# A decoder kernel on one core: the preparation of sparse attention in another order

## What is computed

```python
q, rows, win, gates, qm = nsa_split(hp @ nsa_w_in[j], nsa_gate_b[j])     # 12 query heads, 2 kv heads, head size 128
q = rms_norm(q, nsa_g_q[j])                                              # q / rms(q) * g_q
kc = rms_norm(nsa_compress(rows[:, :, 0], ...), g_k[0])                  # 3 kinds of keys, each normed
ks, kw = rms_norm(rows[:, :, 2], g_k[1]), rms_norm(win_k, g_k[2])
s = einsum(q, k) * HEAD_DIM ** -0.5 + table[t5_bucket(dist)]             # in each of three branches
o = gate_0 * o_cmp + gate_1 * o_sel + gate_2 * o_win                     # gates are sigmoids
```

## Time and profile before

| | us |
|---|---|
| median of three runs | 3449.14 (3446.73 to 3450.45) |
| the profiled execution | 3445.69, of which the span on the core is 3443.8 |
| `prepare_sparse` | from 674.4 to 728.9 |
| `attend_sparse_prompt` | from 728.9 to 815.8 |
| `attend_sampled` | from 815.8 on |
| busy over the span: TensorE, VectorE, ScalarE, GpSimd | 92%, 47%, 37%, 6% |

### The profile page before, as it was taken

How to read it: one execution, slowest core, us unless ns; L and a number is a source line. 1 busy time by engine, 2 the same in 40 slices (tenths; PEclk the granted TensorE clock), 3 DMA queues, 4 the chain that set the end, 5 groups by cost and what they waited for, 6 DMA issues and landing times. The chain is left out here.

```text
span 3443.8 us, 56594 instructions
## 1 busy us (share of the span) xinstructions
PE 3169.4 (92%) x23855; PEld 2974.5 (86%) x23855; DVE 1612.0 (47%) x1681; ACT 1275.7 (37%) x1312; POOL 204.1 (6%) x137
## 2 busy tenths in 40 slices
PE   7899999875679999999999999967699999999999
PEld 6798999844349999999999999944299999999999
DVE  5543444346764544334444444365745443344433
ACT  5432345324763433333332432245034332334332
POOL 0000000003430000000000000025100000000000
PEclk9999999978989999999999999978799999999999
DMA  6556454324754455455555445304644555555553
GB/s 219 156 160 206 139 157 136 122 98 141 234 193 159 146 160 171 160 171 160 170 160 171 149 161 169 106 25 142 214 146 141 166 164 166 165 165 164 165 166 132
DMA packets 317556, 541.82 MB, mean 157 GB/s; under 512 B 18277, under 2 KB 115551, under 8 KB 316136
## 3 DMA queue, kind: packets, MB, share of 16 engines
q1 hardware_dynamic: 316728, 534.45, 48.1%
q10 hardware_dynamic: 624, 4.46, 0.3%
HBM read 519.59 MB, written 27.55 MB: 159 GB/s over the span
## 5 line engine op out<-in xcount | busy, mean ns | idle before, releaser
L516 DVE TENSOR_TENSOR project_weights_low<-ring_x,project_weights_high 128x2048 fp32r<-128x2048 f32 x344 | 788.6, 2292 | 1207.0 <-ACT project_weights_high L444 1206.9
L444 ACT ACTIVATE project_weights_high<-ring_x 128x2048 fp32r<-128x2048 f32 x344 | 658.7, 1915 | 1256.8 <-PE project_banks L372 1256.8
L370 PE MATMUL project_banks<-high,project_weights_high 128*128 128x288 f32 x2560 | 761.6, 297 | 27.6 <-DVE project_weights_low L506 23.8
L371 PE MATMUL project_banks<-low,project_weights_high 128*128 128x288 f32 x2560 | 760.2, 297 | 0.0
L372 PE MATMUL project_banks<-high,project_weights_low 128*128 128x288 f32 x2560 | 759.9, 297 | 0.0
L370 PE MATMUL project_banks<-up_high,project_weights_high 128*128 128x288 f32 x2048 | 605.4, 296 | 0.0
L371 PE MATMUL project_banks<-up_low,project_weights_high 128*128 128x288 f32 x2048 | 605.2, 296 | 0.0
L372 PE MATMUL project_banks<-up_high,project_weights_low 128*128 128x288 f32 x2048 | 605.1, 295 | 0.0
L370 PEld LDWEIGHTS project_banks<-high,project_weights_high 128*128 128x128 f32 x2560 | 486.8, 190 | 29.3 <-DVE project_weights_low L506 24.5
L371 PEld LDWEIGHTS project_banks<-low,project_weights_high 128*128 128x128 f32 x2560 | 486.3, 190 | 0.0
L372 PEld LDWEIGHTS project_banks<-high,project_weights_low 128*128 128x128 f32 x2560 | 485.3, 190 | 0.0
(11 more groups left out here) (516 smaller groups left out, 3021.2 us busy)
## 6 DMA issues: line engine op xcount, KB each, us to landing
ring_x<-in_w_up_dram SPq DMA_DIRECT2D x128, 1024.0 KB, 5.2
ring_x<-in_w_down_dram SPq DMA_DIRECT2D x128, 1024.0 KB, 5.1
ring_x<-in_gla_w_in_dram SPq DMA_DIRECT2D x40, 1024.0 KB, 5.0
h<-in_cache_nsa_kv_dram SPq DMA_DIRECT2D x256, 128.0 KB, 2.3
ring_x<-in_w_out_dram SPq DMA_DIRECT2D x32, 1024.0 KB, 5.1
ring_x<-in_nsa_w_in_dram SPq DMA_DIRECT2D x28, 1024.0 KB, 5.0
ring_x<-in_w_mem_kv_dram SPq DMA_DIRECT2D x16, 1024.0 KB, 5.2
sp_keys_values<-in_cache_nsa_kv_dram SPq DMA_DIRECT2D x64, 256.0 KB, 3.8
```

Of the source, the lines that this page charges most:

```text
L370: nc.tensor.matmul(bank, w_high, moving_high[:, kt], start=(kt == 0), stop=False)
L371: nc.tensor.matmul(bank, w_high, moving_low[:, kt], start=False, stop=False)
L444: nc.scalar.activation(weights_high[:, c % 2], g.ring[:, c % RING], ACT.Copy).then_inc(rounded, 1)
L516: nc.vector.tensor_tensor(weights_low[:, c % 2], g.ring[:, c % RING], weights_high[:, c % 2].bitcast(F32), ALU.subtract).then_inc(split, 1)
```

## The change

In `prepare_sparse` the order of SP's loads is turned round (`near` last). The 24 prompt query tiles are turned by TensorE, in six sets of four placed between the sets of rows, and ScalarE squares each set out of PSUM; VectorE sums them along the free axis, where 24 matmuls did so before. The key squares and their sums come first. The sampled queries are copied to `q_sampled` early and raw; ScalarE squares and multiplies them by the gain. Their inverse norm is applied in `attend_sampled`, where VectorE's additions of a bias become scalar_tensor_tensor with the scale `q_scale_sampled`. The flips come last.

```diff
+        TURNS = [("rows", n) for n in range(4)] + [("queries", n) for n in range(3)] + [
+            ("rows", 4), ("queries", 3), ("rows", 5), ("queries", 4), ("rows", 6), ("queries", 5), ("rows", 7), ("rows", 8)]
 # sync
-            sp.dma_start(g.near[:], ...).then_inc(loaded, 16)
+            sp.dma_start(gate_rows[:], a.gate_rows).then_inc(loaded, 16)
+            sp.dma_start(g.sparse_masks[:], a.sparse_masks).then_inc(loaded, 16)
             sp.dma_start(bias[:], g.bias_dram).then_inc(loaded, 16)
-            sp.dma_start(g.sparse_masks[:], a.sparse_masks).then_inc(loaded, 16)
-            sp.dma_start(gate_rows[:], a.gate_rows).then_inc(loaded, 16)
+            sp.dma_start(g.near[:], ...).then_inc(near_loaded, 16)
...
 # tensor
+            for at, (what, n) in enumerate(TURNS):
+                if at == 3:
+                    pe.wait_ge(k_squared, 1)
+                    for o in range(KEYS):
+                        mm = nc.tensor.matmul(sums_ps[32 * o:32 * o + 32, 3, 0:TOKENS], g.ones[:, 0:32], squares[:, o], ...)
+                    mm.then_inc(k_summed, 1)
+                rows(n) if what == "rows" else queries(n)   # rows waits rows_copied n-3, queries q_squared n-2
+            pe.wait_ge(own_squared, 1)
+            for t in range(PAIRS):
+                mm = nc.tensor.matmul(sums_ps[:, 3, OWN_AT + t:OWN_AT + t + 1], own_squares[:, t], g.ones[:, 0:1], ...)
...
+            pe.wait_ge(k_inverse, 1)
+            pe.wait_ge(q_squared, Q_SETS)
+            pe.wait_ge(q_mean, 1)
+            pe.wait_ge(blank, 1)
+            for o in range(KEYS):
+                mm = nc.tensor.matmul(sums_ps[:, o, 0:TOKENS], spread[:, o], inverse_rms[:], start=True, stop=True)
+            mm.then_inc(spread_done, 1)
+            pe.wait_ge(near_loaded, 16)
             for n in range(FLIPS):   # waits gates_read, scaled, flip_copied 1; banks of rows_ps and sums_ps in turn
...
-            for k in range(HEADS):
-                for i in range(QT):
-                    nc.tensor.matmul(rows_ps[:, 2, k * QT + i:k * QT + i + 1], q_squares[:, k, i * P:(i + 1) * P], ...)
 # scalar
-            nc.scalar.activation(q_squares, g.p[:, 0:HEADS], ACT.Square).then_inc(q_squared, 1)
+            for at, (what, n) in enumerate(TURNS):
+                rows(n) if what == "rows" else queries(n)   # Copy to g.rows, or Square of sums_ps to q_squares
+                if at == 4:
+                    act.wait_ge(own_copied, 1)
+                    nc.scalar.activation(own_squares[:], g.q_sampled[:], ACT.Square).then_inc(own_squared, 1)
+                    act.wait_ge(own_squared, 1)
+                    nc.scalar.activation(g.q_sampled[:], g.q_sampled[:], ACT.Copy, scale=g.vec[:, gq:gq + 1])
+                if at == 6:
+                    act.wait_ge(k_mean, 1)
+                    nc.scalar.activation(inverse_rms[:], inverse_rms[:], ACT.Sqrt).then_inc(k_root, 1)
+            act.wait_ge(q_mean, 1)
+            nc.scalar.activation(q_rms[:], q_rms[:], ACT.Sqrt).then_inc(q_root, 1)
             for n in range(FLIPS):   # copies, now from flip_ps[n]
...
 # vector: neg_bias; key squares; the 16 copies; k_mean; gates; key gains; k_inverse; then
+            for n in range(Q_SETS // 2):
+                dve.wait_ge(q_squared, 2 * n + 2)
+                linked(nc.vector.tensor_reduce(q_rms[:, 8 * n:8 * n + 8], ..., AX_X, ALU.add))
 # then q_mean; gates read; q_scale, q_scale_sampled; the keys scaled (scaled); the bias read; new_k
-            linked(nc.vector.scalar_tensor_tensor(own, own, scaled_gain[:, 0:1], q_rms[:, HEADS * QT:]..., ALU.mult,
-                ALU.mult))
 # attend_sampled, vector (L2146; L2154, L2226, L2232 and L2235 in the same way)
-                linked(nc.vector.tensor_tensor(s_cmp[:], s_ps[:, 0]..., cmp_bias[:]..., ALU.add))
+                for t in range(PAIRS):
+                    last = nc.vector.scalar_tensor_tensor(s_cmp[:, t], s_ps[:, 0, t * P:(t + 1) * P], q_scale(t),
+                                                          cmp_bias[:], ALU.mult, ALU.add)
+                linked(last)
```

More of the change, by code:

```diff
@@ L1398, in _, with rows @@
         def _(pe):
-            for n, (s, tok) in enumerate(sets):
-                if n >= 4:
-                    pe.wait_ge(rows_copied, n - 3)
+            def rows(n):
+                s, tok = sets[n]
+                wait(pe, rows_copied, n - 3)
                 for o in range(4):
@@ L1442, in sum_squares @@
[L1442 to L1461, removed]
@@ L1476, in _ @@
                     g.near[:].rearrange("p h c -> p (h c)").rearrange("p (n b c) -> p n b c", b=FLIP_BANKS, c=512)[:, n],
[L1477 to L1482, removed]
+                    flip_ps[n], ACT.Copy).then_inc(flip_copied, 1)
+            act.wait_ge(own_gained, 1)
         @block.vector
@@ L1504, in _ @@
             nc.vector.tensor_reduce(g.gates_sampled[:], own_gates[:].rearrange(
-                "p (r t c) -> p t r c", t=PAIRS, c=2 * STEP), AX_X, ALU.add)
-            dve.wait_ge(turned, len(sets) + 2)
+                "p (r t c) -> p t r c", t=PAIRS, c=2 * STEP), AX_X, ALU.add).then_inc(gates_read, 1)
+            dve.wait_ge(q_root, 1)
+            linked(nc.vector.reciprocal(q_rms[:], q_rms[:]))
+            nc.vector.tensor_scalar(g.q_scale[:].rearrange("p k i -> p (k i)"), q_rms[:, 0:UNITS], SCALE, None, ALU.mult)
+            nc.vector.tensor_scalar(g.q_scale_sampled[:], q_rms[:, UNITS:], SCALE, None, ALU.mult)
+            dve.wait_ge(spread_done, 1)
+            dve.wait_ge(rows_turned, len(sets))
+            for o, (tile, gain) in enumerate(normed):
+                parts = [(slice(0, SEQ), key_gain[:, gain - gk:gain - gk + 1]),
+                         (slice(SEQ, TOKENS), g.vec[:, gain:gain + 1])]
+                for cols, col in parts:
+                    last = nc.vector.scalar_tensor_tensor(g.p[:, tile, cols], g.p[:, tile, cols], col,
+                                                          sums_ps[:, o, cols], ALU.mult, ALU.mult)
+            last.then_inc(scaled, 1)
+            dve.wait_ge(biased, 1)
             nc.vector.tensor_copy(g.bias_far[:], rows_ps[:, 3, 0:1])
@@ L1516, in _ @@
                     linked(nc.vector.scalar_tensor_tensor(g.bias_near[:], near, at, g.bias_near[:], ALU.mult, ALU.add))
[L1517 to L1536, removed]
@@ L1545, in _ @@
-            for r in range(rounds):
-                dve.wait_ge(root, r + 1)
-                nc.vector.reciprocal(inverse_rms[:, r % 2], inverse_rms[:, r % 2]).then_inc(inverse, 1)
-                dve.wait_ge(spread_done, r + 1)
[L1549 to L1553, removed]
-                    parts = [(slice(0, SEQ), key_gain[:, gain - gk:gain - gk + 1]),
-                             (slice(SEQ, TOKENS), g.vec[:, gain:gain + 1])]
-                    for cols, col in parts:
-                        last = nc.vector.scalar_tensor_tensor(g.p[:, tile, cols], g.p[:, tile, cols], col,
-                                                              sums_ps[:, o, cols], ALU.mult, ALU.mult)
-                last.then_inc(scaled, 1)
@@ L1560, in _ @@
[L1560 to L1568 removed]
+            nc.vector.tensor_scalar(g.bias_far[:], g.bias_far[:], 1.0, None, ALU.mult).then_inc(bias_read, 1)
@@ L2152, in front @@
                 yield -1.5
-                for w in range(2):
-                    last = nc.vector.tensor_tensor(
-                        s_new[:, :, w], s_ps[:, 1, 0:2 * PAIRS * NEW].rearrange("p (t w n) -> p t w n", w=2, n=NEW)[:, :, w],
-                        mask[:, SP_OTHER:SP_OTHER + PAIRS * NEW].rearrange("p (t n) -> p t n", n=NEW), ALU.add)
+                for t in range(PAIRS):
+                    other = mask[:, SP_OTHER + t * NEW:SP_OTHER + (t + 1) * NEW]
+                    last = nc.vector.scalar_tensor_tensor(
+                        s_new[:, t], s_ps[:, 1, 2 * t * NEW:2 * (t + 1) * NEW].rearrange("p (w n) -> p w n", n=NEW),
+                        q_scale(t), other.unsqueeze(1).to_broadcast([P, 2, NEW]), ALU.mult, ALU.add)
                 last.then_inc(small_taken, 1)
```

156 lines of the change are left out of this document (92 added, 64 removed).

## The result

The changed kernel takes 3433.95 us (median of five runs, 3432.71 to 3434.09), the kernel before 3447.59 (five runs, 3444.6 to 3450.45): a ratio of 0.9964, with a 95% interval of 0.9952 to 0.9975. A second series on another chip gave 3434.84 against 3445.59, 0.9969 (0.9957 to 0.9980). The ratio is estimated from the single runs; it makes the gain 12.4 us in the first series and 10.7 in the second, where the medians differ by 13.6 and 10.8. So the change gains 11 to 14 us, 0.3 to 0.4%. The forecast was 7.4 us, and the measured time lies 2 us under the forecast's range.

What follows compares the result with a forecast made beforehand. Window copies from DRAM to DRAM, not compute, were to end the preparation after the change: -8.2 us there, +0.8 us in the sampled stage, so 3449.14 - 7.4 = 3441.7 us, range 3436 to 3447.

Steps and rivals of the forecast that it cites:

- The compute tail hides a DMA tail that is only 13.0 us shorter: Preparation's end: SP released at about 715.65, other engines ending at 728.65; gains beyond 13.0 us do not shorten the stage.
- The compute tail: Preparation, last serial work on the compute engines: to fall from 728.65 to about 708, covered by window copies ending at 720.4.
- The chain that I added up: Preparation: last rows copied 687.7, sampled stores 687.75, window copies 692.15, SP released 720.4, prompt stage at 720.75, 8.2 us earlier.
- ScalarE's fourth copy of rows: Preparation: assumed to start at 679.0, after the key-square sums and the fourth set's turns; last rows copied 8.7 us later.
- eight small stores and one larger one ... 4.4 us: Preparation: SP's issue of the sampled-row stores ahead of the window copies, taken as 687.38 - 682.98 = 4.4 us.
- The prompt stage: Prompt stage: same work, no change taken from 86.9 us; upper clock level would gain at most 5.2 us.
- about 1 us: Prompt stage: possible cost if TensorE's clock rises later, after some 12 us idle instead of 4.3 us.
- The table load's gap: Preparation, ScalarE, rival: gap between table load and square root delays the stage's end equally; 3442.7 at 1 us, chance 0.03.
- The sampled stage: Sampled stage: scalar_tensor_tensor adds 2.6 us of VectorE work, of which +0.8 us was taken to lengthen the stage.
- the share that reaches the end: Sampled stage: half of the longer takes' 1.5 us assumed to lengthen the stage, between ends of 0 and 2.6 us.
- The rival on the slower side: Sampled stage: 28 new scalar_tensor_tensor instructions stall 0.7 us each beside GpSimd, 20 us in all, giving 3461; chance 0.04.
- The step that failed most: the reference level: Whole kernel: -7.4 us applied to the runs' median 3449.14, 3.45 us above the profiled execution's 3445.69, giving 3441.7.

## Why the prediction was wrong

**Right: what ends the stage.** "The compute tail hides a DMA tail that is only 13.0 us shorter" held: SP's final wait for others went from 13.0 to 0.2 us, and taking the copies away uncovered 14.4 us after the change and nothing before it. The compute tail ended 30.7 us into the stage (704.6); I had worked out 31.5 to 36.5 (706 to 711).

**Right but mis-sized: the point of issue.** The chain that I added up, in time since the start of the stage: last rows copied at 13.2 us forecast, 13.9 measured (13.2 in the second profile); window copies issued at 17.7 forecast, 17.0 measured (16.3); next stage at 46.3 forecast, 45.2 measured (44.6, and 44.7 with the reduction doubled). ScalarE's fourth copy of rows, which the sum has at 4.5 us, started at 5.0 and 4.3 us. The term that failed is "eight small stores and one larger one ... 4.4 us": they took 3.1 us in both profiles, since eight stores were issued in 2.65 us instead of 4.00. The timeline of the second profile:

```profile
687.11 2.64 SPq L1387 DMA_DIRECT2D out_nsa_win_sample_dram<-rows_sampled  x8
...
690.16 5.05 SPq L1392 DMA_DIRECT2D out_nsa_win_sample_dram<-in_state_nsa_win_dram  x8
```

I had taken the 4.4 us from stores issued while `near` was under way. Here the rows are ready later and `near` has landed (11.1 us after its issue at 675.1) before the stores are issued at 687.8. The copies ran 27.7 us from issue to release (28.3 forecast). So the preparation gained 9.2 us in the first pair of profiles and 9.6 in the second, where I had summed 8.2.

**The prompt stage.** I had taken no change. It lasted 86.9 and 88.2 us in the changed kernel's two profiles and 87.2 and 86.9 before: at the bottom nothing, at the top the "about 1 us" that I had named for a later rise of the clock.

**The table load's gap.** It did not come. The load and the root that wanted it, in ScalarE's timeline:

```profile
682.22 1.28 ACT L1503 ACT_TABLE_LOAD   x1
683.51 0.44 ACT L1503 ACTIVATE prep_inverse_rms<-prep_inverse_rms 128x288 f32<-128x288 f32 x1
```

0.01 us lies between them. The Trainium skill (ScalarE: Activation LUTs, What ACT_TABLE_LOAD costs) adds a drain of some 1.38 us to each switch; this case's traces show none, and the measurement decides.

**The sampled stage.** Forecast +0.8 us. The mean over three profiles with the old takes is 213.1 us, over six with the new ones 213.8: +0.7, in a scatter of 1 to 2 us. That this agrees is luck: the durations were right, the share that reaches the end was about 0.8 and not half, and the scatter is larger than the difference. The new takes in the changed kernel:

```profile
L2258 DVE SCALAR_TENSOR_TENSOR sp_s<-sp_s_ps,q_scale_sampled,sp_sel_bias 128x512 f32<-128x512 f32 x12 | 8.9, 739 | 0.0
...
L2255 DVE SCALAR_TENSOR_TENSOR sp_s<-sp_s_ps,q_scale_sampled,sp_near_bias 128x128 f32<-128x128 f32 x4 | 1.4, 340 | 0.0
L2166 DVE SCALAR_TENSOR_TENSOR sp_s_cmp<-sp_s_ps,q_scale_sampled,sp_cmp_bias 128x128 f32<-128x128 f32 x4 | 1.1, 345 | 1.1 <-PE sp_s_ps L1984 1.1
```

739 ns against the 751 taken from the prompt stage, 345 against 0.33 us. With 0.77 of 1.5 us it would have been +1.2. The rival on the slower side is dead with the same rows: of the 32 instructions of the new form the longest took 0.75 us, so none of them stalled beside GpSimd.

**The step that failed most: the reference level.** "That execution stands 3.45 us under the median of the runs, so for the median 3449.14 - 7.4". I took the median of three runs as the kernel's level. With two more on the same chip it is 3447.59; sixteen runs on a later chip have a median of 3445.59, fifteen on another 3445.36. So the three had been some 3.6 us high, half the size of the change. The changed kernel took 3433.95 us on the first chip and 3434.84 on the later one, so the first chip isn't slower as such; whether its level for the kernel before is really 2 us higher, five runs can't tell. The forecast of -7.4 from 3445.5 would have been 3438.1; what was measured is 3434 to 3435.

So of the miss of 7.8 us (3441.7 against 3433.95), some 3.6 us are the level, 1.0 to 1.4 us the preparation's length, and the rest, some 3 us, is not settled. For the two profiles that I compared the account closes: their spans differ by 13.0 us, 9.2 in the preparation, 0.2 in the prompt stage, -0.5 in the sampled stage, 3.3 in the linear stages and 0.7 elsewhere, most of it before the preparation starts. The 3.3 us belong to the first profile of the kernel before. What stays open is why the timed runs show more than the stages. By the lengths of stages the changed kernel gains 9.4 us in the preparation and gives back 0.7 in the sampled stage and, in some executions, 1 in the prompt stage; the timed runs say 10.7 and 12.4 (0.9969 and 0.9964), with intervals that reach down to 6.9 and 8.6 us. Part of it is which executions were profiled: the two of the kernel before, and the one of it with the copies later, lie 1.9, 1.8 and 5.9 us under the medians of their timed runs, the two of the changed kernel 1.2 and 0.3. What takes longer in the other executions, no profile shows. The kernel before scatters from 3441.4 to 3448.8 in sixteen runs, seven of the changed one lie within 3.1 us; but the changed kernel with its reduction doubled covers 5.6 us in ten, so that the change narrows the scatter isn't shown.

## What to carry to other kernels

When a chain is to be shortened, read how long the queue engine of the same stage waits for the others at the stage's end: that number, 13.0 us here, is the cap on what shortening the chain alone can give, and it moves if the change touches what the queue's issues wait for. A transfer that nothing in its stage depends on belongs into the stage with an idle DMA queue; done here it is worth 14 to 17 us on top of the change, and without the change nothing that the runs can tell (0.4 to 0.7 us of the stage). And for a change of a few microseconds in three thousand, get the level of the kernel before from many runs and more than one profile before adding anything up.

## What the runs showed of the hardware

- Copies of 1016 KB from DRAM to DRAM, eight issued within 5 us on one queue, moved one after the other: half-microsecond windows of the changed kernel show eight bursts some 3.1 us apart, of about one copy's bytes each, the first and the last but one of them being

```profile
692.00:692.50 0.50, 0.50 (x3) 0.36 (x2) 0.00 (x0) 0.00 (x0) 0.00 (x0) 0.50 4.42 1431
...
711.00:711.50 0.50, 0.00 (x0) 0.00 (x0) 0.00 (x0) 0.00 (x0) 0.00 (x0) 0.50 3.05 1040
```

  and first issue to release was 27.5 to 28.3 us in the six profiles that have the copies at the end of the preparation, and 27.7 us in two with the copies in the prompt stage. The DMA engines' share was 0.90 to 0.96 over these stretches.
- Issuing the eight small stores took SP 2.64 or 2.65 us in five profiles, with a DMA share of 0.2 to 0.5 meanwhile; 3.59 with the rows first (share 0.90); 4.00, 4.32 and 4.42 in the two profiles of the kernel before and the one of it with the copies later (1.00 to 1.04); and 4.62 behind the window copies (1.24). An issue is no constant of 0.5 us; that busy DMA engines slow it fits these numbers but was not tried by itself.
- The 48 instructions at the start of the prompt stage (moving operand of 8 columns) ran for 10.38 us without a gap at a granted clock of 0.50 in the changed kernel. Where the stage began 1.8 us behind the flips and at a clock of 1.00, the clock fell to 0.50 after 0.4 us in one kernel (10.03 us for the 48) and 1.1 us in the other (9.36).
